# A two-layer encoder trunk on one core: attention values with v stationary, a router that works block by block, a longer warm-up and a split tail

## The chip, the cores and the metric

The kernel runs on one core of one Trainium2 chip, in one launch. The metric is the device time in microseconds of that core, the median over several executions. Lower is better.

## What is computed

The input x is 256 tokens of 1024 float32 channels. Two residual layers, each with a token mixer and a channel mixer, and a last RMSNorm:

```python
for i in range(2):
    hn = rms_norm(h, norm_mix[i])
    h = h + (fourier_mixer(hn, w_in, w_out) if i == 0 else neighbourhood_attention(hn, w_qkv, rpb, w_o))
    hn = rms_norm(h, norm_ffn[i])
    h = h + (swiglu(hn, ffn_gate, ffn_up, ffn_down) if i == 0 else moe_swiglu(hn, router_w, router_b, ...))
return rms_norm(h, final_norm)
```

Layer 0 mixes tokens and channels by a 2-D Fourier transform between two 1024x1024 projections, and then has a dense SwiGLU with 2816 hidden channels. Layer 1 has attention with 16 heads of 64 channels and a biased window, and then a mixture of 8 experts (3584 hidden channels each) of which every token takes its top 2. All of it is in float32.

## The kernel before

The program is written engine by engine (one block for each of SyncE, GpSimd, ScalarE, VectorE and TensorE), so the order on every engine is the order of the code, and semaphores join the engines. No scheduler moves anything.

**Weights.** All weights come in pieces of 128x2048 floats (1 MB, `raw`, a ring of 7, loaded by SyncE). For float32 accuracy each piece is split in two: ScalarE writes its rounded part (`w_hi`, L458), VectorE the remainder (`w_lo`, L753), both in rings of three (`SPLIT`). `split_past(n)` in the code of either engine makes all pieces up to n + 2 that aren't made yet. TensorE multiplies each tile in three products (`three`, L1250 to L1252: high by high, high by low, low by high). A piece is 12 products of 512 columns for one block of 128 tokens. Loading piece j waits until piece j - 7 is split.

**Stages.** `still` runs products of zeros (L1321) until the first data is there. Then `first_projection` and w_in, the Fourier transform (`token_dft` into bank T, `channel_dft` into bank Y, each alternating between two of the eight PSUM banks), w_out, the dense feed-forward part, qkv. The left operands `act_hi` and `act_lo` come from transposes of h, a quarter (two of the eight channel tiles) at a time; `stream_second` has TensorE wait for two quarters before it starts on them.

**Attention.** In a loop over 8 pairs of heads TensorE does the scores of pair p (L1512, 64 channels each, so the two heads sit in the upper and lower half of the array), the four transposes per head of the previous pair's probabilities (L1525), and the values of the pair before that (`head_values`, L1537: the transposed probabilities are the stationary operand, 64 columns of v the moving one). VectorE adds the bias (L951) and takes the maximum (L955), ScalarE copies transposed probabilities (`probT`, L625) and takes the exponentials (L630, four for a pair). VectorE divides eight heads at once by their sums (`output`, L933 and L936), and `outputs_transposed` (L1488) turns them by TensorE before the projection w_o (`wo_product`, pieces W0 to W0+3).

**Router.** After the last w_o product the second half of h is transposed for both token blocks, split into act_hi and act_lo, multiplied by the router's weights (L1578, L1585, 8 to 16 columns), and a chain of small VectorE instructions finds the two experts of each token and its slot. `keep_warm` (L1592) is filler: products of the identity with itself. Then the tokens of expert 0 are gathered by products with a 0/1 matrix (L1619), transposed, split, and the first gate product starts.

**Experts and end.** 8 experts of 42 pieces each. The last expert's result is scattered back (L1766, L1767), added to h (L1118), and the last norm and the four stores follow.

Of the kernel before, what the change touches and what calls it, by code (L numbers as in the profile page):

```python
# [26 lines left out]
P = 128  # L27
D = 1024
S = 256
# [96 lines left out]
def trunk(nc, x, norm_mix, norm_ffn, w_in, w_out, w_qkv, w_o, ffg, ffu, ffd, router_w, router_b,  # L126
# [47 lines left out]
    def layout(entries, off):  # L174

        made = {}
        for name, shape, dt in entries:
# [11 lines left out]
                       ("p_sum", [P, NB, HEADS], f32), ("p_inv", [P, NB, HEADS], f32)]  # L189
# [44 lines left out]
    def sem(name):  # L234
# [5 lines left out]
    lo_part, still_made = sem("lo_part"), sem("still_made")  # L240

# [19 lines left out]
    bias_done, a_score, a_biased, a_max, a_exp, a_inv, a_pT, a_pTcopy, a_pv, a_out, a_oT, a_ohi, a_olo, ao_psum = (sem(n) for n in (  # L261
        "bias_done", "a_score", "a_biased", "a_max", "a_exp", "a_inv", "a_pT", "a_pTcopy", "a_pv", "a_out", "a_oT", "a_ohi", "a_olo", "ao_psum"))

    sq_half, before_done, hnr_hi, hnr_lo, rw_hi_done, rw_lo_done, ones_done, logit_psum, low_added, gap_done, ratio_done, used_done, rank_psum, flag_done, dve_chain = (sem(n) for n in (
        "sq_half", "before_done", "hnr_hi", "hnr_lo", "rw_hi_done", "rw_lo_done", "ones_done", "logit_psum", "low_added", "gap_done", "ratio_done", "used_done", "rank_psum", "flag_done", "dve_chain"))
# [4 lines left out]
    e_y, fin_rstd, fin_done = (sem(n) for n in ("e_y", "fin_rstd", "fin_done"))  # L270
# [31 lines left out]

    def has_before(j, E, back):

        return E is not None or j >= back
# [3 lines left out]
    STREAM = [TY, TY, TY, [G[0], G[1], U[0], Y[0]]]  # L309
# [6 lines left out]
    OT = [U[0], Y[0], G[0], G[1]]  # L316
    WO = [[U[0], Y[0]], T]

    def HT(c):

        return G if c == DC - 1 else T

# [11 lines left out]
    def _(sp):  # L334
# [53 lines left out]
        for b in range(NB):  # L388
            for q in range(2):
                sp.wait_ge(fin_done, 2 * b + q + 1)  # L390
                cs = slice(BANK * q, BANK * (q + 1))
                sp.dma_start(out[0, P * b:P * (b + 1), cs], hn[:, b, cs]).then_inc(s_out, 16)
# [3 lines left out]
    def _(pool):  # L396
# [11 lines left out]

        pool.wait_ge(a_pv, HEADS)
# [8 lines left out]
        rstds(3)  # L418
# [22 lines left out]

        for b in range(NB):
            pool.wait_ge(sq_done, NB * 4 + b + 1)
            nc.gpsimd.tensor_scalar(rstd[:, 4, b:b + 1], sumsq[:, 4, b:b + 1], 1.0 / D, EPS, ALU.mult, ALU.add).then_inc(rstd_chain, 1)
            pool.wait_ge(rstd_chain, 4 + 1 + b + 1)
# [3 lines left out]
    def _(act):  # L449
        made = [0]  # L450

        def split_hi(j, E):
# [5 lines left out]
            nc.scalar.activation(w_hi[w][:], raw[s][:], ACT.Copy).then_inc(hi_made, 1)  # L458

# [25 lines left out]
        def squares(i):  # L485
# [3 lines left out]
            for b in range(NB):  # L489
                if i == 4:  # L490
                    act.wait_ge(e_added, b + 1)
                terms = mo["hn_hi"] if i == 4 else hn
# [40 lines left out]
        for g in range(GROUPS + 2):  # L533
            for m in (2 * g, 2 * g + 1) if g < GROUPS else ():
# [3 lines left out]
                nc.scalar.activation(fo["pt_hi"][:, m % PT], T[m % 2][:], ACT.Copy).then_inc(pt_hi_done, 1)  # L538
# [4 lines left out]
            if 1 <= g < GROUPS + 1:  # L543
# [3 lines left out]
                nc.scalar.activation(fo["odd"][:, (g - 1) % 2], Y[(g - 1) % 2][:, S:], ACT.Copy).then_inc(ft_odd, 1)  # L547
# [50 lines left out]
        def output_hi(q):  # L598
            act.wait_ge(a_oT, q + 1)
            nc.scalar.activation(act_hi[:, 2 * q:2 * q + 2], two(OT[q]), ACT.Copy).then_inc(a_ohi, 1)  # L600
# [14 lines left out]
        split_past(W0 - 2)  # L615
        for p in range(PAIRS + 1):
# [3 lines left out]
            if p:  # L620
                for g in (2 * p - 2, 2 * p - 1):
# [4 lines left out]
            if p < PAIRS:  # L626
                for i in (2 * p, 2 * p + 1):
# [9 lines left out]
            if 0 <= p - FIRST_PART < PARTS:  # L637
                split_part(W0 + 1, p - FIRST_PART)
        split_past(W0)
        output_hi(2)  # L640
        output_hi(3)
        split_past(W0 + 1)
        act.wait_ge(s_rout, 64)
        nc.scalar.activation(mo["rw_parts"][:, :, :NE], mo["rw"][:], ACT.Copy).then_inc(rw_hi_done, 1)
        split_past(W0 + 3)
        stream_hi(3, 0)

        def token_hi(c):

            cs = slice(BANK * c, BANK * (c + 1))  # L650
            for b in range(NB):
# [1184 lines left out]
```

## Time and profile before

| | |
|---|---|
| median of 3 executions | 1366.86 us (1364.64 to 1367.56) |
| the profiled execution's own time | 1367.15 us |
| its span in the trace | 1365.3 us |
| TensorE busy | 1344.7 us, 98% |
| VectorE busy | 1111.9 us, 81% |
| ScalarE busy | 923.2 us, 68% |
| GpSimd busy | 34.5 us, 3% |
| data moved | 432.32 MB, 317 GB/s on average |

A busy time is the union of an engine's instructions, with the ends of TensorE's pipelined instructions modelled; so the distance between starts tells more of TensorE than its busy share. Times in the rows below are from the start of the span.

### The profile page before, as it was taken

The numbers are of one execution on the slowest core, as the hardware profiler recorded it, in microseconds if no ns is written. First come the engines' busy times: TensorE is split into PE (matmuls) and PEld (weight loads), VectorE is DVE, ScalarE is ACT, GpSimd is POOL, SyncE is SP. The second block draws the span as 40 slices with busy tenths as digits, with TensorE's granted clock in tenths as the row PEclk, the third lists the DMA queues.
The fourth block names the chain that finished last, engine by engine and source line by source line (L and its number), as shares of the span: only waits on it lengthen the run. The fifth ranks groups of instructions, "written<-read, shape, count | busy, mean of one in ns | idle before, by whom it ended". The sixth has DMA issues, their size and how long they took to land.

```text
span 1365.3 us, 17406 instructions
## 1 busy us (share of the span) xinstructions
PE 1344.7 (98%) x6341; PEld 1117.9 (82%) x6341; DVE 1111.9 (81%) x815; ACT 923.2 (68%) x755; POOL 34.5 (3%) x48
## 2 busy tenths in 40 slices
PE   8999999999999999999999999999999999999997
PEld 7888888787878888888888888888888888888885
DVE  5756666655678889888988988898898889889997
ACT  6554444545647778777777877877787787777774
POOL 0000000000101000000000000000000000002000
PEclk8999999999989999999999999999999999999999
DMA  9666775563339999999999999999999999999992
GB/s 354 246 207 179 210 211 190 175 204 104 101 109 378 383 378 365 395 382 357 398 388 372 373 394 377 358 398 388 368 376 394 367 370 397 381 374 385 396 394 90
DMA packets 194971, 432.32 MB, mean 317 GB/s; under 512 B 19632, under 2 KB 22064, under 8 KB 194800
## 3 DMA queue, kind: packets, MB, share of 16 engines
q1 hardware_dynamic: 178784, 416.28, 83.4%
q0 software_dynamic: 3360, 11.78, 2.2%
q10 hardware_dynamic: 12784, 3.69, 1.8%
q8 instruction: 27, 0.44, 0.1%
q14 instruction: 16, 0.13, 0.0%
HBM read 425.94 MB, written 5.78 MB: 316 GB/s over the span
## 4 chain that ended last, share of the span: by engine, by line
PE 95%; DVE 3%; ACT 1%; issue 1%; DMA 0%; POOL 0%; DVEq 0%; ACTq 0%
PE bank_G L1250 10%; PE bank_G L1252 10%; PE bank_G L1251 10%; PE bank_U L1250 10%; PE bank_U L1252 10%; PE bank_U L1251 10%; PE bank_Y L1250 8%; PE bank_Y L1252 8%; PE bank_Y L1251 8%; PE bank_T L1696 2%; PE bank_T L1250 1%; PE bank_T L1252 1%; PE bank_T L1251 1%; DVE w_lo L753 1%; PE bank_G L1512 0%
## 5 line engine op out<-in xcount | busy, mean ns | idle before, releaser
L753 DVE TENSOR_TENSOR w_lo<-raw,w_hi 128x2048 fp32r<-128x2048 f32 x390 | 885.9, 2289 | 184.6 <-ACT w_hi L458 183.8
L458 ACT ACTIVATE w_hi<-raw 128x2048 fp32r<-128x2048 f32 x390 | 748.6, 1920 | 276.6 <-PE bank_U L1252 98.2
L1250 PE MATMUL bank_Y<-w_hi,hidT_hi 128*128 128x512 f32 x492 | 192.2, 391 | 0.0
L1252 PE MATMUL bank_Y<-w_hi,hidT_lo 128*128 128x512 f32 x492 | 191.6, 389 | 0.0
L1251 PE MATMUL bank_Y<-w_lo,hidT_hi 128*128 128x512 f32 x492 | 191.5, 389 | 0.0
L1250 PE MATMUL bank_U<-w_hi,xg_hi 128*128 128x512 f32 x448 | 179.1, 400 | 0.0
L1250 PE MATMUL bank_G<-w_hi,xg_hi 128*128 128x512 f32 x448 | 175.2, 391 | 1.3 <-DVE xg_lo L774 0.9
L1252 PE MATMUL bank_U<-w_hi,xg_lo 128*128 128x512 f32 x448 | 175.0, 391 | 0.0
L1251 PE MATMUL bank_U<-w_lo,xg_hi 128*128 128x512 f32 x448 | 174.5, 390 | 0.0
L1252 PE MATMUL bank_G<-w_hi,xg_lo 128*128 128x512 f32 x448 | 174.5, 390 | 0.0
L1251 PE MATMUL bank_G<-w_lo,xg_hi 128*128 128x512 f32 x448 | 174.4, 389 | 0.0
L1252 PEld LDWEIGHTS bank_Y<-w_hi,hidT_lo 128*128 128x128 f32 x492 | 92.4, 188 | 19.4
L1250 PEld LDWEIGHTS bank_Y<-w_hi,hidT_hi 128*128 128x128 f32 x492 | 92.3, 188 | 19.3
L1251 PEld LDWEIGHTS bank_Y<-w_lo,hidT_hi 128*128 128x128 f32 x492 | 92.4, 188 | 18.7
L1250 PEld LDWEIGHTS bank_G<-w_hi,xg_hi 128*128 128x128 f32 x448 | 84.1, 188 | 21.0 <-issue 2.9
L1252 PEld LDWEIGHTS bank_U<-w_hi,xg_lo 128*128 128x128 f32 x448 | 84.1, 188 | 18.3
L1252 PEld LDWEIGHTS bank_G<-w_hi,xg_lo 128*128 128x128 f32 x448 | 84.1, 188 | 17.7
L1251 PEld LDWEIGHTS bank_G<-w_lo,xg_hi 128*128 128x128 f32 x448 | 84.1, 188 | 17.1
L1251 PEld LDWEIGHTS bank_U<-w_lo,xg_hi 128*128 128x128 f32 x448 | 84.3, 188 | 16.3
L1250 PEld LDWEIGHTS bank_U<-w_hi,xg_hi 128*128 128x128 f32 x448 | 84.2, 188 | 15.9
L1250 PE MATMUL bank_G<-w_hi,act_hi 128*128 128x512 f32 (+1 forms) x176 | 68.6, 390 | 4.4 <-DVE w_lo L761 3.1
L1250 PE MATMUL bank_U<-w_hi,act_hi 128*128 128x512 f32 (+1 forms) x176 | 67.7, 384 | 0.3 <-DVE act_lo L774 0.3
(301 smaller groups left out, 1363.5 us busy)
## 6 DMA issues: line engine op xcount, KB each, us to landing
raw<-in_expert_w_gate SPq DMA_DIRECT2D x112, 1024.0 KB, 7.7
raw<-in_expert_w_up SPq DMA_DIRECT2D x112, 1024.0 KB, 7.8
raw<-in_expert_w_down SPq DMA_DIRECT2D x112, 1024.0 KB, 7.7
raw<-in_nat_w_qkv SPq DMA_DIRECT2D x12, 1024.0 KB, 5.1
raw<-in_ffn_w_gate SPq DMA_DIRECT2D x11, 1024.0 KB, 8.9
raw<-in_ffn_w_up SPq DMA_DIRECT2D x11, 1024.0 KB, 5.7
raw<-in_ffn_w_down SPq DMA_DIRECT2D x11, 1024.0 KB, 5.2
raw<-in_fourier_w_out SPq DMA_DIRECT2D x4, 1024.0 KB, 15.6
```

The costliest lines, as they stand in the source:

```text
L458: nc.scalar.activation(w_hi[w][:], raw[s][:], ACT.Copy).then_inc(hi_made, 1)
L753: nc.vector.tensor_tensor(w_lo[w][:], raw[s][:], w_hi[w][:].bitcast(f32), ALU.subtract).then_inc(lo_made, 1)
L1250: nc.tensor.matmul(out_, xh, wh, start=start, stop=False)
L1251: nc.tensor.matmul(out_, xh, wl, start=False, stop=False)
L1252: return nc.tensor.matmul(out_, xl, wh, start=False, stop=stop)
L1696: last = nc.tensor.transpose(T[c % 2][:, P * k:P * (k + 1)], hid[c % 2][:, P * k:P * (k + 1)], ident[:])
```

## The change

- `still(12)` becomes `still(23)`.
- The Fourier transform uses four banks for `token_dft` (BY_TOKEN) and four for `channel_dft` (BY_CHANNEL), and drops the waits that two banks needed.
- For gate column 0 and qkv column 0, TensorE waits for one quarter of `act_lo` at a time.
- Attention values: v (64 columns) is stationary and the transposed probabilities (256 columns) move, so the result of a pair comes out with channels on partitions, the two heads in the two halves of the partitions. The reciprocals of the sums (VectorE) are spread over 64 columns by GpSimd (`p_wide`), transposed by TensorE (two per pair), copied by ScalarE (`scale_copy`), and multiplied by VectorE (`scaled_values`). `outputs_transposed` is gone. ScalarE now alternates one probT copy and one head's two exponentials.
- Router: h is added, transposed, squared, split and multiplied for one block of tokens after the other; w_o products change their order. The gains are multiplied into the router's weights. Two weight pieces less are split ahead of the router. `keep_warm(6)` becomes 24, `keep_warm(2)` becomes 8.
- End: the last piece of the last expert is split in halves by columns; the first half of the result is scattered and added while the second is computed. The squares are taken by halves, and the last scaling is shared by VectorE and ScalarE.

```diff
-        still(12)
+        still(23)
...
-            if m >= 2:
-                pe.wait_ge(pt_lo_done, m - 1)
+            if m >= 4:
+                pe.wait_ge(pt_lo_done, m - 3)
...
+                        if stream is not None and b == 0 and kk % 2 == 0:
+                            pe.wait_ge(act_lo_done, 4 * stream + kk // 2 + 1)
...
+        for p in range(PAIRS):
+            pool.wait_ge(a_inv, p + 1)
+            if p >= 2:
+                pool.wait_ge(a_rT, p - 1)
+            nc.gpsimd.tensor_copy(att["p_wide"][:, p % 2].rearrange("p b (h d) -> p b h d", h=2),
+                                  att["p_inv"][:, p % 2].unsqueeze(3).to_broadcast([P, NB, 2, HD])).then_inc(a_wide, 1)
...
+        def pair_values(p):
+
+            pe.wait_ge(a_pTcopy, 2 * p + 2)
...
+            if p >= 2:
+                pe.wait_ge(a_out, p - 1)
+            for k in range(NB):
+                for half in range(2):
+                    g = 2 * p + half
+                    last = nc.tensor.matmul(values_of(p)[HD * half:HD * (half + 1)], att["v"][:, k, HD * g:HD * (g + 1)],
+                                            att["probT"][:, g % PROBS, S * k:S * (k + 1)], start=(k == 0), stop=(k == NB - 1))
+            last.then_inc(a_pv, 2)
+            pe.wait_ge(a_wide, p + 1)
...
+                last = nc.tensor.transpose(scales_of(p)[:, P * b:P * (b + 1)], att["p_wide"][:, p % 2, b], ident[:])
+            last.then_inc(a_rT, 1)
...
-        keep_warm(6)
+        keep_warm(24)
...
-        keep_warm(2)
+        keep_warm(8)
...
+                last_columns(0, 4)
+                last_columns(1, 2)
+                scatter(0)
+                last_columns(1, 2, 2)
```

On ScalarE, two passes through the attention loop, before: `hid` is the exponentials' output, `probT` the copies, `w_hi` a part of a weight piece.

```order
L625 ACTIVATE probT<-bank_T 128x512 x2
L630 ACTIVATE hid,p_sum<-silu_g,neg_max 128x256 x4
L470 ACTIVATE w_hi<-raw 128x512
L625 ACTIVATE probT<-bank_T 128x512 x2
L630 ACTIVATE hid,p_sum<-silu_g,neg_max 128x256 x4
L470 ACTIVATE w_hi<-raw 128x512
```

And the same place after the change:

```order
L661 ACTIVATE scale<-bank_U 128x256
L675 ACTIVATE probT<-bank_T 128x512
L680 ACTIVATE hid,p_sum<-silu_g,neg_max 128x256 x2
L675 ACTIVATE probT<-bank_T 128x512
L680 ACTIVATE hid,p_sum<-silu_g,neg_max 128x256 x2
L512 ACTIVATE w_hi<-raw 128x512
```

The second copy of a pass now stands between the exponentials of the two heads, and a copy of 256 columns is added.

On TensorE, from the last router product to the first gather product, before and after (`ident` alone is the filler, `used` the ranking of the tokens):

```order
L1585 MATMUL bank_G<-rw_parts,act_lo 128x8 x8
L1592 MATMUL bank_T<-ident 128x128 x6
L1610 MATMUL bank_T<-used,before_h 128x8
...
L1614 MATMUL bank_T<-used,ones 128x8
L1592 MATMUL bank_T<-ident 128x128 x2
L1619 MATMUL bank_G<-hn_hi,sel 128x512 x2
```

```order
L1677 MATMUL bank_G<-rw_parts,act_lo 128x8 x4
L1685 MATMUL bank_T<-ident 128x128 x24
L1717 MATMUL bank_T<-used,before_h 128x8
...
L1721 MATMUL bank_T<-used,ones 128x8
L1685 MATMUL bank_T<-ident 128x128 x8
L1726 MATMUL bank_G<-hn_hi,sel 128x512 x2
```

The filler ahead of the ranking grows from 6 products to 24, that behind it from 2 to 8.

On VectorE, behind the router, where the first gate's left operand (`xg_lo`) is made, before and after:

```order
L774 TENSOR_TENSOR xg_lo<-bank_U,xg_hi 128x512
L1201 TENSOR_REDUCE most<-bank_T 128x1
L753 TENSOR_TENSOR w_lo<-raw,w_hi 128x2048
L1205 SCALAR_TENSOR_TENSOR hn<-h,rstd,gain 128x1024 x2
L753 TENSOR_TENSOR w_lo<-raw,w_hi 128x2048
```

```order
L853 TENSOR_TENSOR xg_lo<-bank_U,xg_hi 128x512
L1301 TENSOR_REDUCE most<-bank_T 128x1
L825 TENSOR_TENSOR w_lo<-raw,w_hi 128x2048 x2
L1305 SCALAR_TENSOR_TENSOR hn<-h,rstd,gain 128x1024 x2
L825 TENSOR_TENSOR w_lo<-raw,w_hi 128x2048
```

One more weight piece (W0+5, the second of expert 0) is split here than before; it stood ahead of the router.

## Rows read from the trace of the kernel before

**Rows 1.** The page: shares of the chain that ended last.
```profile
PE 95%; DVE 3%; ACT 1%; issue 1%; DMA 0%; POOL 0%; DVEq 0%; ACTq 0%
```

**Rows 2.** Stretches: us, busy time of each engine, granted clock, DMA share, GB/s.
```profile
385.00:390.00 5.00, 3.56 (x29) 3.15 (x28) 4.49 (x13) 3.41 (x11) 0.54 (x2) 1.00 0.50 197
390.00:404.00 14.00, 12.28 (x59) 10.69 (x59) 9.02 (x33) 4.32 (x7) 1.26 (x2) 0.63 0.01 2
404.00:1354.00 950.00, 949.58 (x4328) 785.49 (x4326) 849.96 (x524) 719.92 (x482) 23.25 (x21) 1.00 1.00 372
```

**Rows 3.** Stretches at the start: L1321 alone (PE, PEld), then all PE.
```profile
1.00:4.33 3.33, 3.23 (x15) 3.23 (x16) 1.00 0.71 218
4.33:5.60 1.27, 1.24 (x11) 1.05 (x10) 1.00 0.72 187
...
7.75:14.57 6.82, 5.92 (x14) 0.50 1.06 405
14.57:22.30 7.73, 7.73 (x35) 1.00 1.03 388
```

**Rows 4.** Timeline around the Fourier transform, VectorE and PE.
```profile
27.67 4.68 DVE L753 TENSOR_TENSOR w_lo<-raw,w_hi 128x2048 fp32r<-128x2048 f32 x2
34.88 1.36 DVE L774 TENSOR_TENSOR pt_lo<-bank_T,pt_hi 128x512 fp32r<-128x512 f32 x2
37.15 0.28 PE L1250 MATMUL bank_Y<-pt_hi,dft_hi 128*128 128x256 f32 x1
```

**Rows 5.** PE's waits of 250 to 265 us: total, times, longest.
```profile
PE bank_G L1250 <- DVE act_lo L778: 1.4, 1, 1.4
```

**Rows 6.** Four attention pairs as one stretch; then timeline rows of one pair.
```profile
337.00:352.18 15.18, 15.18 (x129) 13.41 (x129) 11.87 (x20) 14.12 (x44) 0.00 (x0) 1.00 0.01 2
...
338.06 1.29 DVE L951 SCALAR_TENSOR_TENSOR silu_g<-bank_G,bias 128x512 f32<-128x512 f32 x2 [1.56 <-PE bank_G L1512]
338.65 1.09 ACT L625 ACTIVATE probT<-bank_T 128x512 f32<-128x512 f32 x2
339.27 1.27 DVE L955 TENSOR_REDUCE neg_max<-silu_g 128x2 f32<-128x512 f32 x2
339.98 0.51 ACT L630 ACTIVATE hid<-silu_g,neg_max 128x256 f32<-128x256 f32 x1 [0.24 <-DVE neg_max L955]
```

**Rows 7.** Timeline of PE: scores, transposes, one block's values, first w_o product.
```profile
348.36 1.13 PE L1512 MATMUL bank_G<-kT,qT 64*128 64x256 f32 x8
...
356.78 0.56 PE L1537 MATMUL bank_U<-v,probT 128*128 128x64 f32 x4
358.52 1.04 PE L1525 MATMUL bank_T<-ident,hid 128*128 128x128 f32 x8
359.84 0.50 PE L1250 MATMUL bank_U<-w_hi,act_hi 128*128 128x512 f32 x1 [0.28 <-DVE act_lo L774]
```

**Rows 8.** GpSimd's first instruction of 256 columns in the timeline.
```profile
0.74 0.31 POOL L404 MEMSET hid<- 128x256 f32 x1 [0.29 <-POOLq L1817]
```

**Rows 9.** Timeline of the router, PE and the last VectorE step of the choice.
```profile
385.40 0.51 PE L1578 MATMUL bank_G<-rw_parts,act_hi 128*128 128x16 f32 x4
393.09 2.91 PE L1592 MATMUL bank_T<-ident 128*128 128x128 f32 x12
396.39 0.17 DVE L1029 TENSOR_TENSOR used<-first,second 128x16 bf16<-128x16 f32 x1
398.17 1.22 PE L1619 MATMUL bank_G<-hn_hi,sel 128*128 128x512 f32 x2 [0.19 <-DVE sel L1074]
403.58 0.47 PE L1250 MATMUL bank_G<-w_hi,xg_hi 128*128 128x512 f32 x1 [0.90 <-DVE xg_lo L774]
```

**Rows 10.** VectorE's timeline behind the router.
```profile
404.14 2.29 DVE L753 TENSOR_TENSOR w_lo<-raw,w_hi 128x2048 fp32r<-128x2048 f32 x1
406.35 2.47 DVE L1205 SCALAR_TENSOR_TENSOR hn<-h,rstd,gain 128x1024 f32<-128x1024 f32 x2
```

**Rows 11.** VectorE's timeline at the end.
```profile
1359.98 2.74 DVE L1236 SCALAR_TENSOR_TENSOR hn<-h,rstd,gain 128x512 f32<-128x512 f32 x4 [1.42 <-POOL rstd L446]
```

More of the change, by code:

```diff
@@ L619, in _ @@
                 output_hi(1)
-            if p:
-                for g in (2 * p - 2, 2 * p - 1):
+            if p >= 3:
+                scale_copy(p - 3)
+            for half in range(2):
+                if p:
+                    g = 2 * p - 2 + half
                     act.wait_ge(a_pT, g + 1)
@@ L625, in _ @@
                     nc.scalar.activation(att["probT"][:, g % PROBS], T[g % 2][:], ACT.Copy).then_inc(a_pTcopy, 1)
-            if p < PAIRS:
-                for i in (2 * p, 2 * p + 1):
+                if p < PAIRS:
+                    i = 2 * p + half
                     act.wait_ge(a_max, i + 1)
@@ L967, in _ @@
         split_past(W0)
-        for b in range(NB):
-            output(1, b)
+        scaled_values(PAIRS - 2)
+        scaled_values(PAIRS - 1)
         output_lo(2)
@@ L1177, in expert @@
                         gather_copy(E + 2)
+                if (kind, c, half) == ("up", STEPS - 1, 0) and kept and not sweep:
+                    gate_weights()
                 if (kind, half) == ("down", 0) and kept and not sweep and 1 <= c < 5:
@@ L1252, in three, with project @@
             return nc.tensor.matmul(out_, xl, wh, start=False, stop=stop)
-        def project(pieces, banks, width, done, before=lambda n, b: None):
+        def project(pieces, banks, width, done, before=lambda n, b: None, stream=None):
             for n, j in enumerate(pieces):
@@ L1340, in token_dft @@
             for b in range(NB):
-                last = three(T[m % 2][:, S * b:S * (b + 1)], fo["u_hi"][:, b, o:o + P], fo["u_lo"][:, b, o:o + P],
+                last = three(BY_TOKEN[m % 4][:, S * b:S * (b + 1)], fo["u_hi"][:, b, o:o + P], fo["u_lo"][:, b, o:o + P],
                              fo["dft_hi"][:, b, 0:S], fo["dft_lo"][:, b, 0:S], True, True)
@@ L1480, in v_product @@
                 last.then_inc(qkv_psum, 1)
[L1482 to L1489 removed]
         def wo_product(c, half, b):
             pe.wait_ge(a_olo, 2 * half + 2)
+            if (c, half) == (0, 0):
+                pe.wait_ge(a_out, PAIRS - 3 + b)
             last = quarter(at["wo"][c][half], half, b, WO[c][b])
@@ L1592, in keep_warm, with last_wo_product @@
                 nc.tensor.matmul(T[0][:, :P], ident[:], ident[:], start=True, stop=True)
-        pe.wait_ge(rw_lo_done, 1)
-        pe.wait_ge(act_lo_done, 4 * 3 + 2)
-        for q in range(2):
-            logits_hi(q)
-            logits_lo(q)
-        transpose_stream(3, 1)
-        logits_hi(2)
-        logits_hi(3)
-        logits_lo(2)
-        logits_lo(3).then_inc(logit_psum, 1)
-        keep_warm(6)
+        def last_wo_product():
+            j = at["wo"][1][1]
+            ready(j, None)
+            wh, wl = parts(j, None, KH)
+            for k in range(KH):
+                if k == KH // 2:
+                    transpose_tokens_of(1, 0)
+                kk = KH + k
+                last = three(WO[1][1][:], act_hi[:, kk, P:], act_lo[:, kk, P:], wh[:, k], wl[:, k], False, kk == KD - 1)
+            last.then_inc(piece_used, 1)
+        wo_product(0, 1, 0)
+        wo_product(1, 1, 0)
+        transpose_tokens_of(0, 0)
+        wo_product(0, 1, 1)
+        transpose_tokens_of(0, 1)
+        last_wo_product()
+        pe.wait_ge(rw_lo_done, 1)
+        logits(0, 0)
+        logits(0, 1)
+        transpose_tokens_of(1, 1)
+        logits(1, 0)
+        logits(1, 1)
+        keep_warm(24)
         pe.wait_ge(used_done, 1)
```

392 lines of the change are left out of this document (230 added, 162 removed).

## The prediction

> **What bounds the kernel now.** I read the chain that ended last first: TensorE holds 95% of it [rows 1]. Then the stretches: from 404 to 1354 us, 70% of the span, TensorE is busy 949.58 of 950 us at full clock [rows 2]; and the change touches nothing in it. There a piece is 12 products of 512 columns, at about 0.225 us each (35 records begin in 7.73 us in [rows 3], and a few records can be missing), 2.7 us. So only TensorE's gaps and its half-clock stretches elsewhere can be won or lost. They are five: the start, the Fourier transform, one wait at 256 us, the attention stage with the router behind it, and the end. In each I ask which engine's result TensorE waits for, and what is late next when that wait is taken away. The sum below is made against the profiled execution's own 1367.15 us, which is 0.3 above the median.
>
> **Start and Fourier transform: −2.2.** Before, 24 filler instructions (two for each product) run from 1.1 us on, up to 4.33 at half clock (15 in 3.23 us, 0.213 each), then at full (11 in 1.24 us, 0.11 each; a stretch counts what crosses its border); then TensorE idles from 5.6 to 8.65 us, where the first weight piece is ready. The 14 products from 7.75 to 14.57 run at 0.50 of the clock, those behind at full clock [rows 3]; so 14 cost 14 × 0.21 = 2.9 us more. `still(23)` issues 46 instructions: 15 × 0.213, and 31 × 0.11 = 3.4, so it ends near 7.8 and leaves 0.9 us idle. Before, the clock was still full 2.2 us after the filler ended, so I take it as full from the first product on. That moves TensorE about 3 us ahead, but the next consumer is limited by VectorE: it makes two pieces of `w_lo` from 27.67 on, 4.68 us, and only later the first `pt_lo`, 34.88 to 36.24, without which the channel transform can't begin (37.15) [rows 4]. That VectorE work waits for TensorE only through `u_lo`, so it moves by about 1.3 us at the first `pt_lo` (ready 34.9 instead of 36.2); the four banks then take away a further 0.9 us of bank waits. I book 2.2 of at most 3.2. The bounds: 0 if the clock falls in the 0.9 us and VectorE stays where it is, −3.2 if nothing behind TensorE is late.
>
> **Quarter waits: −0.8.** TensorE waits 1.4 us for `act_lo` at 256.6 [rows 5]. The four instructions that make it (0.41 us each) are waited for as four; waiting for the first two saves two of them, 0.8. The bounds are 0 and −1.4. At qkv the same wait has slack already, so nothing.
>
> **Attention, steady pairs: 0.** Four pairs take 15.18 us, all TensorE; ScalarE has 14.12 of it busy [rows 6]. So a pair takes 3.8: scores 1.06, eight transposes 0.95 to 1.04, values 358.52 − 356.78 = 1.74 for four groups [rows 7]. After the change the values are eight instructions of 256 columns. In the trace 128 columns of such a product take 0.11 [rows 3], so one after another they would take 8 × 0.22 = 1.8, as before. But the scores are eight instructions of 256 columns too, and take 1.13 [rows 7], because the upper and the lower half of the array work at once. If the left and the right half do the same, the values take about 1.0, and with the two transposes of `p_wide` (0.28) TensorE's pair falls to 3.3. The Trainium skill's page "TensorEngine Tiling (Array Packing)", section Performance Considerations, names this very exchange, a small moving side made stationary together with column tiling, with up to 2× to be had. The same page, Key Properties, speaks against it: a change of tiling mode drains TensorE, and there would be one more change in each pair. By the first rule the values would take about 0.9, by the second some of it comes back; this case has a row for row halves only, and no run here shows column halves yet.
>
> What a pair can give is not TensorE's, though. Bias (0.65 a head), maximum (0.64), exponential (0.51 twice) and copy (0.55) hang in a ring [rows 6]: the bias of pair p + 1 writes `silu_g`, which the exponentials read. Before, the order is bias, maximum, two copies in the maximum's shadow, four exponentials. After, a copy stands between the two heads' exponentials: 0.6 + 0.65 + 1.0 + 0.5 + 1.0 and handovers of 0.24 or less are 3.95, above the 3.8 of before. Five pairs lose 0.13 each, the first pair wins 0.6 (no values in it, no pair of copies): 0.
>
> GpSimd's spreading of the reciprocals is hidden. It has no row; the nearest is its write of 256 columns, 0.31 us [rows 8], and its slack is a whole pair less two handovers, about 1.6 us. Above 1.6 each microsecond would delay a pair.
>
> **From scores(7) to the logits: +0.6.** Before, the first product with w_o starts 7.66 us after scores(7) (352.18 to 359.84) [rows 7]. After, bias of the last head starts 2.2 us after the scores do, and then stand in line 0.6 (bias), 0.7 (maximum), 1.0, 0.5, 1.0 (exponentials, copy, exponentials), 1.0 (`act_hi` twice, each as a copy of 512 columns), 0.4 (`scale_copy`), 0.4 (product with v's result), 0.1 (reciprocal) and 1.3 (`act_lo` twice, as `pt_lo`): 9.2 us, +1.5. The 0.4's are guesses between 0.31 and 0.55, as no row has 256 columns of these forms. Then it gives back: the values of heads 14 and 15 −0.55, no `outputs_transposed` in the second half −1.0; and three groups of four transposes now stand between w_o products where one of eight stood behind them, +0.65. The sum is +0.6. If the column halves do not overlap, 1.9 must be added.
>
> **Router: +0.2.** With t0 the end of the last w_o product (385.40), before has the logits at t0 + 7.9, `used` at 396.56, the ranking at t0 + 11.2, the gather at t0 + 12.8, the first gate product at t0 + 18.2 [rows 9]. At 390.04 the clock fell, and stayed at half to 400.28 (0.63 as a mean of the stretch to 404, 1.00 ahead of it [rows 2]). After, the logits are there at t0 + 4.8, since the transposes, splits and squares of block 0 lie behind w_o's own products, and the chain of small VectorE instructions (2.9 us) has `used` at t0 + 7.8. But TensorE first runs 48 filler instructions: 5.3 us at 0.11, 10.2 at 0.213 (12 took 2.91, which has two handovers in it [rows 9]). If the clock falls in the middle of them they take 7.75, the ranking starts at t0 + 12.5, the second filler (16) takes 1.8 and the gather starts at t0 + 14.4. From gather to gate were 5.4 us; 1.4 of them is the half clock up to 400.28, so 4.0 remain: t0 + 18.4. So the gain of the logits (3.1 us) goes into filler that is longer than the work it covers.
>
> **Expert 0: +1.5.** VectorE after the router has one `w_lo` of 2.29 us, then `hn` twice, 2.47 us, then the next `w_lo` [rows 10]. After the change two pieces are split ahead of `hn`, W0+5 and W0+6, so W0+7, the fourth of the expert, is ready at 0.56 + 2 × 2.21 + 2.47 + 2.29 = 9.7 behind the gate's start (VectorE begins 0.56 behind it, and the pieces' starts are 2.21 apart), and TensorE wants it three pieces behind it, at 8.2. Before the slack was 0.7. Wait 1.5. If VectorE starts it while TensorE still gathers, 0.7; bound 2.3.
>
> **End: −0.8.** The adds end 0.5 later by halves, but the squares behind them are taken half by half, and the last scaling (four in 2.74 us on VectorE [rows 11]) is shared with ScalarE: −1.3.
>
> **Sum:** 1367.15 − 2.2 − 0.8 + 0.6 + 0.2 + 1.5 − 0.8 = 1365.65 for the profiled execution, and 0.3 less against the median: 1365.4.
>
> **The rivals.**
> A. As above: 1365.4, with 1363.6 to 1366.8 by half the terms' bounds. For it speaks that the clock fell at t0 + 4.6 before, with TensorE idle in pieces ahead of it (3.56 busy of 5 us [rows 2]), which the new order leaves in part. Chance 0.40.
> B. The clock holds all through the router, because the w_o products, transposes and filler follow each other without idle time: filler 5.3, ranking at t0 + 10, gate at t0 + 15.8, −2.6 on A: 1362.8. Against it: the products of 8 and 16 columns keep TensorE's clock no longer than 4.6 us in the trace of before. Chance 0.25.
> C. The column halves do not overlap, or each change of shape costs what the overlap gives: +1.9, 1367.3. For it: no row shows them overlapping. Against it: row halves do. Chance 0.20.
> D. Slower than before: the clock is half through the whole filler and the gather. Then ranking at t0 + 15, gather at t0 + 18.4, gate at t0 + 23.8: +5.4 on A, 1370.8. Each filler instruction at half clock costs 0.1 more: from 15 more than in A the kernel is no longer faster, and only with all of both fillers and part of the gather at half (+4.3) is it slower by over 0.2%. Chance 0.15.
> GpSimd as the bound of the pairs (over 2 us a spreading) is in D's chance, too, at +1 to +2 in eight pairs.
>
> **Numbers.** A measurement of this kernel tells from no change about 0.2%, 2.7 us. Faster by that (under 1364.1): most of B and a third of A, 0.36. Slower by that (over 1369.6): most of D, 0.14. The rest, 0.50. The range leaves out 1 in 10 on either side: from B's lower part, 1360.8, to between C and D, 1368.8.
>
> **What would show it.** At the start: clock 1.00 from 7.75 to 14.57, and the first channel product near 35. At 256: a wait of 0.6. In attention: pairs 3.95 apart, value instructions 0.11 to 0.14 apart if halves overlap and 0.22 if not, and the w_o gap at scores(7) + 9.2. In the router: `used` long done when the ranking starts, the filler its releaser, and the place of the clock's fall. In expert 0: a wait of about 1.5 on `w_lo` before the fourth piece. At the end: last `hn` 0.8 closer to the last product. Most likely to make me wrong is the clock in the router, 5 us from best to worst; next the overlap of the halves, 1.9.

## The result and the profile after

| | before | changed kernel |
|---|---|---|
| median | 1366.82 us (20 executions) | 1369.22 us (20 executions) |
| lowest and highest | 1364.64, 1368.03 | 1367.35, 1370.16 |
| profiled execution, its span | 1367.15, 1365.3 | 1367.38, 1365.6 |

The ratio is 1.0019 with a 95% interval of 1.0012 to 1.0025: 1.6 to 3.4 us slower, where a gain of 1.4 was forecast. The changed kernel's executions fall into two groups, five from 1367.35 to 1367.80 and fifteen from 1368.75 to 1370.16. The mean granted clock is on record for each: 0.996 or 0.997 in the five, 0.995 in eleven of the fifteen and 0.996 in four. The profiled one is of the lower group, so its trace doesn't show what the median has; the profiles of the variants do (below). One of the eleven executions of e8 (below) took 1687.20 us at a mean granted clock of 0.75, and its ratio leaves it out.

The table follows TensorE through three traces: before, the changed kernel (lower group), and e7 (below), the same kernel but for who issues two stores, profiled in the upper group. Times are starts in the timeline.

| start of | before | changed | e7 |
|---|---|---|---|
| first channel product | 37.15 | 34.42 | 34.95 |
| first qkv product | 258.36 | 254.93 | 255.46 |
| scores(0) | 320.20 | 316.77 | 317.29 |
| scores(7) | 352.18 | 349.01 | 349.54 |
| first w_o product | 359.84 | 358.22 | 358.75 |
| last w_o product | 385.17 | 382.76 | 384.85 |
| ranking | 396.62 | 394.75 | 396.83 |
| first gate product | 403.58 | 401.09 | 403.18 |
| 37th product with xg_hi (fifth piece) | 415.93 | 415.05 | 417.11 |
| end of the span | 1365.26 | 1365.57 | 1367.92 |

The changed kernel is 3.4 us ahead at the scores, 2.5 at the first gate product, 0.9 in the fifth piece of expert 0, and 0.3 behind at the end. The start: the stretches that answer to [rows 3], TensorE alone.

```profile
7.75:14.57 6.82, 6.82 (x38) 1.00 1.06 405
14.57:22.30 7.73, 7.73 (x36) 1.00 1.03 388
```

The products there run at full clock now. The attention's last passes, in the timeline (start, duration, engine, line, operation, count, and in brackets the idle time before and who ended it); [rows 6, 7] show the same of before.

```profile
347.63 1.08 PE L1633 MATMUL bank_U<-probT,v 128*64 128x256 f32 x8
348.64 0.44 PE L1640 MATMUL bank_U<-ident,p_wide 128*128 128x128 f32 x2
349.01 1.14 PE L1606 MATMUL bank_G<-kT,qT 64*128 64x256 f32 x8
350.05 0.40 POOL L434 COPY p_wide<-p_inv 128x256 f32<-128x256 f32 x1 [3.57 <-DVE p_inv L1012]
...
354.01 1.08 PE L1633 MATMUL bank_U<-probT,v 128*64 128x256 f32 x8 [0.95 <-ACT probT L675]
354.85 1.14 ACT L640 ACTIVATE act_hi<-hn 128x512 fp32r<-128x512 f32 x2
355.30 1.04 PE L1619 MATMUL bank_T<-ident,hid 128*128 128x128 f32 x8
356.28 0.42 DVE L1017 TENSOR_TENSOR hn<-bank_Y,scale 128x256 f32<-128x256 f32 x1 [2.92 <-ACT scale L661]
356.70 1.46 DVE L853 TENSOR_TENSOR act_lo<-hn,act_hi 128x512 fp32r<-128x512 f32 x2
358.22 0.50 PE L1352 MATMUL bank_U<-w_hi,act_hi 128*128 128x512 f32 x1 [1.89 <-DVE act_lo L853]
```

Eight value products of 256 columns take 1.08 us. In the trace they start in pairs, 0.01 us apart, and a pair follows the other after 0.21 to 0.26: the left and the right half of the array do work at once. Still, scores(6) and (7) start 3.97 us apart where it was 3.82, and TensorE waits twice before the w_o product. The stretches that answer to [rows 2], all engines (PE, PEld, DVE, ACT, POOL, granted clock, DMA, GB/s):

```profile
350.00:358.22 8.22, 5.10 (x38) 3.08 (x36) 4.87 (x10) 7.55 (x22) 1.58 (x3) 1.00 0.41 131
358.22:366.00 7.78, 7.78 (x38) 5.81 (x39) 4.34 (x5) 3.06 (x5) 3.38 (x6) 1.00 0.39 120
382.99:388.62 5.63, 5.01 (x45) 4.91 (x44) 3.23 (x10) 3.23 (x4) 1.64 (x3) 1.00 0.00 0
388.62:392.04 3.42, 3.42 (x18) 3.42 (x18) 2.00 (x13) 1.69 (x2) 0.00 (x0) 0.50 0.01 2
392.04:401.09 9.05, 8.15 (x68) 7.41 (x66) 4.32 (x11) 1.44 (x3) 0.00 (x0) 1.00 0.01 2
```

TensorE is busy 5.10 of the 8.22 us ahead of the w_o product. The router's rows, which answer to [rows 9]:

```profile
387.68 7.23 PE L1685 MATMUL bank_T<-ident 128*128 128x128 f32 x48
390.75 0.17 DVE L1127 TENSOR_TENSOR used<-first,second 128x16 bf16<-128x16 f32 x1
394.75 0.17 PE L1717 MATMUL bank_T<-used,before_h 128*128 128x8 bf16 x1
396.66 0.71 PE L1726 MATMUL bank_G<-hn_hi,sel 128*128 128x512 f32 x2
401.09 0.47 PE L1352 MATMUL bank_G<-w_hi,xg_hi 128*128 128x512 f32 x1 [0.90 <-DVE xg_lo L853]
```

`used` is there at 390.92, and the ranking starts 3.8 us later, with no wait shown: TensorE is still in its own filler. TensorE's waits from 350 to 420 us (in all, times, longest) add the one in expert 0, to set beside [rows 10]:

```profile
PE bank_U L1352 <- DVE act_lo L853: 1.9, 1, 1.9
PE bank_U L1352 <- DVE w_lo L825: 1.0, 1, 1.0
```

And the end, where [rows 11] stood; L1335 multiplies by the gain, L1338 and L809 scale by `rstd`:

```profile
1356.76 0.75 DVE L1216 SCALAR_TENSOR_TENSOR h<-bank_T,weight,h 128x512 f32<-128x512 f32 x1 [0.88 <-PE bank_T L1859]
1358.20 1.29 DVE L1335 TENSOR_TENSOR hn<-h,gain 128x512 f32<-128x512 f32 x2
1358.44 1.10 POOL L478 TENSOR_SCALAR rstd<-sumsq,sumsq_half 128x1 f32<-128x1 f32 x1 [1.71 <-ACT hn_hi L805]
1360.23 0.77 DVE L1338 SCALAR_TENSOR_TENSOR hn<-h,rstd,gain 128x512 f32<-128x512 f32 x1 [0.74 <-POOL rstd L480]
1360.55 0.86 POOL L480 TENSOR_TENSOR rstd<-rstd,half_power 128x1 f32<-128x1 f32 x1
1361.03 2.03 SPq L413 DMA_DIRECT2D out<-hn  x4
1361.45 0.75 DVE L1338 SCALAR_TENSOR_TENSOR hn<-h,rstd,gain 128x512 f32<-128x512 f32 x1 [0.45 <-POOL rstd L480]
1361.51 0.72 ACT L809 ACTIVATE hn<-hn,rstd 128x512 f32<-128x512 f32 x1 [0.49 <-POOL rstd L480]
```

The last hn is ready at 1362.23, 0.5 earlier than before, and yet the span ends 0.3 later. But the kernel came to its end 0.9 ahead: counted from the 37th product with xg_hi, the last hn is 0.4 later than before. The first store is issued at 1361.03, before at 1360.77; counted the same way, it is 1.1 later.

### The profile page after: what moved, and what is told of

Read it like the earlier page. It is cut to its first block, busy times and chain, and to the rows that moved or that the text cites. A ratio compares the mean times of both kernels' runs of the same rounds, so it can differ in the third digit from the quotient of the medians.

```text
span 1365.6 us, 17478 instructions
## 1 busy us (share of the span) xinstructions
PE 1344.4 (98%) x6347; PEld 1111.2 (81%) x6347; DVE 1113.0 (82%) x823; ACT 926.3 (68%) x766; POOL 37.6 (3%) x59
## 4 chain that ended last, share of the span: by engine, by line
PE 92%; DVE 3%; ACT 2%; DMA 1%; issue 1%; SPq 0%; POOL 0%; POOLq 0%; DVEq 0%; ACTq 0%
PE bank_U L1352 10%; PE bank_G L1352 10%; PE bank_U L1354 10%; PE bank_U L1353 10%; PE bank_G L1354 10%; PE bank_G L1353 10%; PE bank_Y L1352 8%; PE bank_Y L1354 8%; PE bank_Y L1353 8%; PE bank_T L1803 2%; DVE w_lo L825 1%; DMA raw<-in_fourier_w_in 1%; PE bank_T L1354 1%; PE bank_T L1352 1%; PE bank_T L1353 1%
## 5 line engine op out<-in xcount | busy, mean ns | idle before, releaser
L1354 PEld LDWEIGHTS bank_U<-w_hi,xg_lo 128*128 128x128 f32 x448 | 84.1, 188 | 18.3
```

The source lines that it names most:

```text
L1354: return nc.tensor.matmul(out_, xl, wh, start=False, stop=stop)
```

## The experiments

Each kernel is the changed one with one edit, timed in several rounds beside the kernel before. Ratios are to the kernel before; the changed kernel's is 1.0019.

**e1: the end of before.** Pieces, adds, squares and scaling as in the kernel before; the core of it:

```diff
-                last_columns(0, 4)
-                last_columns(1, 2)
-                scatter(0)
-                last_columns(1, 2, 2)
+            down(STEPS - 1, 0)
+            down(STEPS - 1, 1)
```

> The changed kernel with the end of the kernel before (last piece whole, adds, squares and last scaling as before). The prediction's theory: the new end saves 0.8 us, so undoing it gives 1369.2 + 0.8 = 1370.0. Theory read from the two traces: from the fourth gate piece of expert 0 on, the changed kernel is 0.88 us ahead and at the end of the span 0.31 behind, so the new end costs 1.2 us, because the last two halves of hn are ready within 0.03 us of each other and their stores are issued one behind the other on SyncE; undoing it gives 1368.0, and the span ends about 2.5 us behind the last hn, not 3.3.

Median 1368.27, ratio 1.0013 (1.0004 to 1.0022), so the interval overlaps the changed kernel's. The trace tells more: from the 37th product with xg_hi to the end of the span are 949.18 us, 949.33 in the kernel before, and 950.52 in the changed one (950.46 to 950.80 in the six variants that keep its end unchanged). The new end costs 1.1 to 1.6 us, against a forecast gain of 0.8.

**e2: `still(12)` again.**

```diff
-        still(23)
+        still(12)
```

> The changed kernel with still(12) again. Theory: the longer filler gives 2.7 us at the first channel product, of which 0.9 belongs to the four banks; undoing the filler costs 1.8 to 2.7, so 1371.0 to 1371.9. The executions of the changed kernel fall into two groups, 1367.4 to 1367.8 and 1368.8 to 1370.2. If the groups come from the clock in the router, both stay, 1.7 us apart. Rival: they come from whether the clock survives the start's filler; then one group is left.

1369.69, ratio 1.0022 (1.0013 to 1.0031). The first channel product starts at 34.94 with the short filler, and in the other variants with the long one and four banks at 34.79 to 35.36. So the filler moves the w_in products (the Fourier transform begins at 31.86, in the others by 31.4) and nothing behind them, within what is measured. Two groups of executions remain, two of eleven in the lower. I expected 1.8 to 2.7 us and that was wrong.

The profile is of the upper group. The w_o products take 24.50 us at full clock; the clock is half in the router, for 6.83 us instead of the changed kernel's 3.41. From the last w_o product to the first gate product are 19.94 us instead of 18.33:

```profile
387.84:394.67 6.83, 6.83 (x34) 6.83 (x34) 2.61 (x15) 2.97 (x3) 0.00 (x0) 0.50 0.00 1
```

**e3: a shorter filler ahead of the ranking.**

```diff
-        keep_warm(24)
+        keep_warm(10)
```

> The changed kernel with 10 filler products ahead of the ranking instead of 24. Theory: the filler is what the ranking waits for (used is done at 390.92, the ranking starts at 394.75), so it starts 3.5 us earlier and the time is 1369.2 - 3.5 = 1365.7. Rival: the clock stays at half through the gather, which takes back 1.5 to 2: 1367.4. Rival 2: with 28 instructions less the clock falls in all executions for two stretches, and nothing is gained in the upper group: 1369.

1366.41, ratio 0.9997 (0.9988 to 1.0006), clear of the changed kernel's interval: 0.22% or 3.0 us by the ratios. The ranking starts at 393.38, right behind `used` (393.06). Its profile also shows what the changed kernel's own didn't. Stretches of e3 around the first w_o products, then the middle one of them in the changed kernel:

```profile
359.00:360.00 1.00, 1.00 (x5) 0.82 (x6) 0.07 (x1) 0.90 (x1) 0.00 (x0) 1.00 0.00 0
360.00:363.41 3.41, 3.41 (x11) 2.20 (x11) 2.56 (x2) 0.00 (x0) 0.00 (x0) 0.50 0.00 0
363.41:366.00 2.59, 2.59 (x16) 1.81 (x17) 0.66 (x2) 1.18 (x3) 1.25 (x2) 1.00 0.84 279
```

```profile
360.00:363.41 3.41, 3.41 (x20) 2.23 (x19) 2.24 (x3) 0.71 (x2) 0.79 (x1) 1.00 0.15 14
```

TensorE is busy all through, but in e3 at the lower of its two clocks (0.50, 1.2 GHz) for 3.4 us, behind the stretch in which it waited twice: 11 products begin there, 20 in the changed kernel. From the first to the last w_o product are 24.54 us in the changed kernel and 26.05 in e3: 1.5 us. The medians of the two groups are 1.7 apart (1367.63 and 1369.36).

**e4: W0+5 split while VectorE waits for the ranking.**

```diff
         nc.vector.tensor_tensor(mo["gap"][:], ...)
+        split_past(W0 + 3)
```

> The changed kernel with piece W0+5 split on VectorE right behind used and gap, where VectorE is idle until the ranking at 394.75. Theory: the wait of 1.2 us on w_lo before the fourth piece of expert 0 and the 0.2 before the second go away and nothing else moves: 1369.2 - 1.4 = 1367.8. Rival: the split's 2.3 us make hn_lo or the slots late: 1369.2 or more. Rival 2: the wait only moves to a later piece of expert 0 and nothing is gained: 1369.2.

1367.78, ratio 1.0012 (1.0003 to 1.0021). The wait on `w_lo` is gone from the trace, and from the first gate product to the 37th with xg_hi pass 12.37 us instead of 13.96, as before the change (12.35). The 1.4 expected is what the medians give; the ratios' intervals overlap.

**e5: filler in the gap ahead of w_o.**

```diff
         head_transposes(HEADS - 1)
+        for _ in range(8):
+            nc.tensor.matmul(G[1][:, 3 * P:4 * P], ident[:], ident[:], ...)
         wo_product(0, 0, 0)
```

> The changed kernel with 8 filler products (identity by identity) behind the last transposes of the attention, where TensorE waits 2.1 us for act_lo before the first product with w_o. Nothing waits less. Theory: in most executions of the changed kernel the clock falls to half for 3.4 us around 359 to 363, just behind that wait (seen in three of four profiles of its variants, not in its own), and costs 1.6 us; with the filler it doesn't fall, the upper group of executions is gone, and the median is 1369.2 - 1.6 = 1367.6. Rival: the clock falls because of the earlier wait too (1.2 us at 353); then the two groups stay and the median is 1369.2.

1369.17, ratio 1.0017 (1.0008 to 1.0026): no gain, and two groups as before. Its profile, of the upper group, shows the clock full behind the first w_o product and then half in the router for twice as long as in the changed kernel, as e2's does:

```profile
358.63:366.00 7.37, 7.37 (x36) 5.48 (x37) 4.35 (x5) 2.65 (x5) 2.97 (x5) 1.00 0.35 101
386.25:393.07 6.82, 6.36 (x30) 6.27 (x30) 3.65 (x18) 4.47 (x5) 0.66 (x1) 0.50 0.01 4
```

Whether the filler kept the clock up there can't be told from one profile, as the changed kernel and e2 had it full there without. The theory (a gain of 1.6) fell: the second half-clock stretch is in this execution all the same, in the router. The rival's number is right, but its reason, that the clock falls in the tail, isn't what the profile shows.

**e6: the left operand of w_o earlier.**

```diff
-        scaled_values(PAIRS - 3)
-        pair_scales(PAIRS - 1)
         output_lo(0)
         output_lo(1)
+        scaled_values(PAIRS - 3)
+        pair_scales(PAIRS - 1)
```

and on ScalarE `output_hi(0)` moves between the last pair's exponentials.

> The changed kernel with act_hi and act_lo of the first four channel tiles made earlier: ScalarE copies the first in the idle 0.67 us ahead of the last pair's exponentials, VectorE makes both act_lo ahead of the scaling of pair 5. Theory: the wait of 2.1 us before the first w_o product is an order on ScalarE and VectorE and not a need; the product starts right behind the transposes, about 1.9 us earlier, and the clock doesn't fall either: 1369.2 - 1.9 - 1.6 = 1365.7, if the w_o stage behind it has no wait of its own. Rival: the w_o stage waits for pieces of w_lo or for the second half of act_lo instead; then only the clock's 1.6 is won: 1367.6.

1367.36, ratio 1.0007 (0.9998 to 1.0016). The w_o product starts at 356.84, 7.2 us behind scores(7), not 9.2, and there is no wait on `act_lo` ahead of it. So that wait was an order on two engines and no need. By the ratios 1.6 us came of the 3.5 expected, with intervals that overlap: the executions still spread from 1365.73 to 1369.71. The profile, one of the three fastest (to 1365.99, the next is 1366.95), has 3.41 us of half clock, all in the router.

**e7: two of the stores issued by ScalarE.**

```diff
+            act.wait_ge(fin_scaled, b + 1)
+            nc.scalar.dma_start(out[0, P * b:P * (b + 1), BANK:], hn[:, b, BANK:]).then_inc(s_out, 16)
```

> The changed kernel with the two stores of the second column half issued by ScalarE behind its scaling instead of by SyncE. Theory: the new end is late because two halves are ready at once and SyncE needs about 0.7 us from one store to the next; with two queues the span ends 0.7 us earlier: 1368.5. Rival: the rest of the end's cost is in GpSimd's chain of three steps for the two rstd (1.1 us for the first), and the store's own time of 2.5 us behind the last hn is the same: 1369.2.

1370.05, ratio 1.0027 (1.0017 to 1.0038), and in the trace 3.33 us from the last hn to the end, as with one queue (3.34). My theory of e1, one store queued behind the other on SyncE, fell.

**e8: two banks each for the Fourier transform, and their waits.**

```diff
-            if m >= 4:
-                pe.wait_ge(pt_lo_done, m - 3)
+            if m >= 2:
+                pe.wait_ge(pt_lo_done, m - 1)
```

> The changed kernel with two banks each for token_dft and channel_dft again, and their waits. Theory: with still(12) the first channel product started at 34.94, within what still(23) gave (34.42 to 35.15), so the filler gives nothing and the banks about 0.9 of bank waits: 1370.1. Rival: the banks give the whole 2.1 us of the start: 1371.3. Rival 2: VectorE is the limit either way, and nothing is lost: 1369.2.

1370.13, ratio 1.0027 (1.0018 to 1.0036), 1.1 us above the changed kernel by the ratios, though the intervals overlap. The first channel product starts at 35.64.

**e9: the last half of hn 0.7 us later.** The added copy's result is not used.

```diff
             act.wait_ge(fin_rstd, b + 1)
+            if b:
+                nc.scalar.activation(mo["hn_hi"][:, b, BANK:], hn[:, b, BANK:], ACT.Copy, ...)
```

> The changed kernel with one more copy of 512 columns (0.7 us, its result unused) on ScalarE ahead of the last scaling, so the last half of hn is ready 0.7 us later and the first three are not. Theory from e7 and the traces: the four stores are 1.05 MB, and from the issue of the first to the end of the span 4.49, 4.54 and 4.55 us pass whatever the last hn does, so the end is set by the first half of hn and nothing changes: 1369.2, span minus first issue 4.55. Rival: the last half of hn sets the end: 1369.9 and 5.3.

Ratio 1.0019 (1.0010 to 1.0028), as the changed kernel. The last hn is ready 2.73 us ahead of the end instead of 3.34, and from the first issue to the end are 4.54 us:

```profile
1363.40 2.17 SPq L413 DMA_DIRECT2D out<-hn  x4
```

The stores' transfers show why. In both traces they begin 0.86 us behind the first issue and fill the DMA engines without a break until 0.8 us before the end. The changed kernel, then e9; the last two figures are the DMA share and GB/s:

```profile
1361.89:1364.78 2.89, 0.00 (x0) 0.00 (x0) 0.31 (x1) 0.34 (x1) 0.00 (x0) 0.50 0.94 363
```

```profile
1364.26:1367.15 2.89, 0.00 (x0) 0.00 (x0) 0.31 (x1) 0.95 (x2) 0.00 (x0) 0.50 0.94 363
```

So the last half of hn had 0.6 us to spare; the first store, with the transfers behind it, set the end.

**e10: four edits together.** e6, the end of before, `keep_warm(10)` and `keep_warm(4)`, and hn of block 0 made ahead of `tokens_lo(1, 1)`:

```diff
         squares_of_rest(1)
...
+        nc.vector.scalar_tensor_tensor(out=hn[:, 0], in0=h[:, 0], scalar=rstd[:, 3, 0:1], in1=mo["gain"][:, 0], ...)
         tokens_lo(1, 1)
```

> The changed kernel with four things undone or moved: act_hi and act_lo of the first channel tiles early (as e6), filler of 10 and 4 products instead of 24 and 8 (as e3), the end of the kernel before (as e1), and hn of the first token block made on VectorE ahead of the last router operand, where VectorE waits 1.3 us, instead of between two weight pieces of expert 0. Theory: the single results, each against its own runs of the kernel before, add up: the changed kernel is 2.4 above it, e6 takes 1.9, e3 2.5, e1 0.7, and hn 1.1 (the wait on w_lo shrinks from 1.2 to about 0.35): 3.8 us below the kernel before, 1363.0. Rival: the changes meet on the same waits, and half of it comes: 1365.

1360.78, ratio 0.9956 (0.9943 to 0.9970): 6.0 us faster than the kernel before, 2.2 more than expected. Of the expected sum only e6, e3 and e1 had been measured; the earlier hn was an estimate, and `keep_warm(4)` never ran alone. The router of e10:

```profile
387.26 4.49 PE L1679 MATMUL bank_T<-ident 128*128 128x128 f32 x20
391.58 0.17 PE L1711 MATMUL bank_T<-used,before_h 128*128 128x8 bf16 x1
...
392.91 0.73 PE L1720 MATMUL bank_G<-hn_hi,sel 128*128 128x512 f32 x2
397.34 0.47 PE L1346 MATMUL bank_G<-w_hi,xg_hi 128*128 128x512 f32 x1 [0.90 <-DVE xg_lo L844]
```

From ranking to gather pass 1.3 us, with 16 filler instructions it was 1.9 to 2.2; from the first gate product to the 37th with xg_hi 12.77. The ranking starts 1.1 us behind `used` (390.51), for the filler still outlasts it.

Beside e7's trace, which has the changed kernel's stages in the upper group, the 8.5 us come as follows: scores(7) to the first w_o product 2.0, the w_o products at full clock 1.6, from the last of them to the first gate product 2.5, from there to the 37th with xg_hi 1.2, the end 1.5, less 0.3 of a later start.

**e11: as e10 with 2 and 2 filler products.**

> As e10 with 2 and 2 filler products. Theory: the ranking can't start before used is made, 3.4 us behind the logits, so less filler only makes TensorE idle there, the clock stays at half longer, and the gather takes 1 to 1.5 us more: 1 to 1.5 above e10. Rival: the filler doesn't matter once it is shorter than the work on VectorE: as e10.

1360.74, ratio 0.9956 (0.9942 to 0.9969): the time of e10, as the rival said. The trace is another. From TensorE's last filler to the ranking are 2.9 us (starts at 386.89 and 389.78), and the ranking starts right behind `used` (389.72), 1.8 us earlier than in e10. But the clock is half until 394.35, through the gather (in e10 until 391.48), and from gather to gate product pass 5.92 us instead of 4.43. So the loss that the theory expected is there, 1.5 us, and the earlier ranking pays for it: that the times are equal is two amounts that cancel.

**e12: e10 with ScalarE's old order**, both copies and then four exponentials.

```diff
                     nc.scalar.activation(att["probT"][:, g % PROBS], T[g % 2][:], ACT.Copy).then_inc(a_pTcopy, 1)
...
+            for half in range(2):
                 if p < PAIRS:
```

> As e10, with ScalarE's old order in the attention loop: both copies of transposed probabilities, then the four exponentials. Theory of the prediction: the copy between the two heads' exponentials is what makes a pair 3.95 to 3.98 us long (bias, maximum, two exponentials, copy, two exponentials in a ring); without it a pair takes 3.8, bounded by ScalarE's own work, and five pairs and the way to the first w_o product give 0.8 to 1.5 us: 1359.3 to 1360.0. Rival: TensorE then waits for the copies, which come no earlier than before while its values start behind them, and a pair stays at 3.97: 1360.8.

1359.69, ratio 0.9946 (0.9933 to 0.9960), the lowest median here, 7.4 us below the kernel before; the interval overlaps e10's. Two passes of PE and ScalarE in its timeline:

```profile
344.99 1.13 PE L1601 MATMUL bank_G<-kT,qT 64*128 64x256 f32 x8
...
347.35 1.09 ACT L671 ACTIVATE probT<-bank_T 128x512 f32<-128x512 f32 x2
...
348.70 1.13 PE L1601 MATMUL bank_G<-kT,qT 64*128 64x256 f32 x8
```

A pair takes 3.71 us, 3.97 with the copy between the exponentials, and 3.82 in the kernel before. The w_o product starts 1.6 us earlier than in e10, but the w_o products then take 25.12 us instead of 24.50, and at the end of the span 0.7 us is left.

## Why the prediction was wrong

It forecast 1365.4 and faster; the kernel takes 1369.2. Two steps failed: the end, booked at −0.8, costs 1.2, and the sum has one stretch of half clock behind the attention where most executions have two, 1.5 us more. Step by step, in the trace of the profiled execution:

- **Start, −2.2:** −2.7 in this execution, −2.0 to −2.4 in most variants. The size held, the working didn't: with the short filler the same start came (e2), where VectorE goes from two weight pieces (27.50 to 32.37) through `u_lo` to `pt_lo` without a wait for TensorE; before, it waited 1.19 us for `u_hi`. Banks give about 1.1 of it by the ratios, whose intervals overlap (e8; its first channel product is 0.3 to 1.2 later than the others'). In e2 the clock was at half for 3.4 us at the start and in the profile of before for 6.8 with the same filler, so part of the 2.2 may be that one execution of before; that stays open. The kernel before isn't one time either: of its 33 executions beside e1, those with a mean clock of 0.994 took 1364.4 to 1366.3 us, those with 0.992 (as the profiled one) 1366.6 to 1367.7.
- **Quarter wait, −0.8:** from the first channel product to the first qkv product −0.7.
- **Steady pairs, 0:** scores(0) to scores(7) took 32.24 instead of 31.98, +0.3. The ring was the right bound (3.95 forecast, 3.97 measured), and e12 shows it by taking the copy out. The win of 0.6 booked against it was 0.3.
- **Scores(7) to the logits, +0.6:** first w_o product 9.2 behind scores(7), as forecast to 0.1; w_o gave 0.8 back. Together +0.8 at full clock.
- **Column halves:** they overlap (eight in 1.08 us): a pair of products every 0.21 to 0.26 us, about what the prediction reckoned for one (0.22). The Trainium skill's page "TensorEngine Tiling (Array Packing)", section Performance Considerations, lists this exchange with 2× column tiling, and the trace agrees. From the last value product to `p_wide` are 0.31 us, 0.1 more than from pair to pair; no experiment separates what that pays for. The Trainium skill says on the same page, section Key Properties, that a change of tiling mode drains TensorE, and this may be its price here. The new order has two more such changes in a pass (into the values and out of them), not the one that the prediction counts.
- **Router, +0.2:** last w_o product to the first gate product 18.33 instead of 18.41, with the filler as what the ranking waited for, and the clock down once in its middle: forecast right in its sum, with luck, as two parts cancel. The ranking came 0.7 earlier than forecast (11.8 behind the end of the last w_o product, not 12.5), and from gather to gate product were 4.4, not 4.0: the prediction took 1.4 off for the half clock from 398.17 to 400.28, and 2.1 us at half clock can cost 1.1 at most. The filler's price is now known: e3 makes it 3.0 us of needless filler.
- **Expert 0, +1.5:** +1.6 (13.96 instead of 12.35), undone by e4. The fourth piece starts 9.7 behind the gate's start, as forecast.
- **End, −0.8: the first step that failed.** It cost 1.2. The +0.5 for the adds held (0.48, counted from the 37th product with xg_hi). Of the −1.3 behind them the halved squares gave 0.4 and the shared scaling 0.8, as booked; but a path that the sum has at nothing took 1.1 back: GpSimd's roots, for which the scaling waits. From the last square to the last root are 2.48 us instead of 1.40, as GpSimd's chain began with a step of 1.10 us that took 0.19 before (read from the two traces; no run changed this chain alone). So the last hn comes 0.4 later behind the same work, not 0.8 earlier.

  The other 0.8 is the stores': from the last hn to the end 3.34 us instead of 2.53, since the prediction timed the last half of hn alone. The end has two limits: the last hn plus 2.5 us (2.53 in before, 2.50 and 2.51 in e1 and e10, whose first issue is 5.0 before the end), and the issue of the first store plus 4.5 (4.54 to 4.55 in the changed kernel, e7 and e9, whose last hn is 2.7 to 3.3 before it; 4.53 to 4.69 in the others with that end). The kernel before met both at once (2.53, 4.49); e12 meets neither closely (2.74, 5.24).

  In the new end the first store comes 1.1 later behind the same work and the last hn 0.4. Where the first store loses its 1.1 is at the scatter (y by selT) around the last product, first before, then changed:

```profile
1353.93 0.39 PE L1252 MATMUL bank_Y<-w_hi,hidT_lo 128*128 128x512 f32 x1
1354.46 0.47 PE L1766 MATMUL bank_T<-y_hi,selT 128*128 128x512 f32 x1
1355.73 0.50 PE L1766 MATMUL bank_T<-y_hi,selT 128*128 128x512 f32 x1
```

```profile
1351.96 0.47 PE L1858 MATMUL bank_T<-y_hi,selT 128*128 128x512 f32 x1
1354.12 0.40 PE L1354 MATMUL bank_Y<-w_hi,hidT_lo 128*128 128x512 f32 x1
1356.02 0.47 PE L1858 MATMUL bank_T<-y_hi,selT 128*128 128x512 f32 x1 [1.50 <-DVE y_lo L853]
```

  Before, the first half's four scatter products ran in the 1.80 us between the start of the last product and the second half's scatter, while `y_lo` was made; now they stand ahead of the last products, and of the same 1.90 us TensorE idles 1.50. So everything on block 0's path is 1.1 later, and from the end of its last add to the first store are 3.52 us in both traces: the halved squares and the shared scaling gave that path nothing.
- **The clock behind scores(7): the second, one half-clock stretch too few.** The sum has the clock fall once, in the router. It priced the new wait ahead of w_o at its 1.5 us and put a fall there at nothing. The profiles of the two lower groups (the changed kernel's and e6's) have one such stretch of 3.41 us from scores(7) to the first gate product. Those of e1 to e5, e8 and e9, all from the upper group of their executions, and that of e7, whose executions show no lower group, have two. In six (e1, e3, e4, e7 to e9) one of the two is in the w_o products, which take 26.0 to 26.1 us instead of 24.5; in e2 and e5 both are in the router, and from the last w_o product to the first gate product are 19.9 and 19.5 us instead of 18.3. The mean clocks of the executions agree: one stretch more lowers the mean by 0.5 × 3.41 / 1366 = 0.0012, and 0.9966 and 0.9953 are the averages of the two groups. Fifteen of twenty executions of the changed kernel are in the upper.

The two, +2.0 and +1.5 in most executions, are 3.5 of the 3.8 us that separate 1369.2 from 1365.4; the pairs' 0.3 is most of the rest. Shown are the 1.2 of the end (e1, and its parts in the two traces) and the price of the second stretch, 1.2 to 1.6, in the traces that have it. What brings it stays open. The wait ahead of w_o is the suspect for its place: of eight profiles that keep that wait without filler six have the fall behind it, of the five others none. But filler in the wait (e5) left the median where it was, without the wait (e6) only three of eleven executions are in the lower group (to 1365.99, the others from 1366.95), and e10 to e12 have two stretches in the router. That e10 gave more than was expected is, by the stretches, mostly the w_o products at full clock, 1.6 us; which of its edits did that wasn't taken apart.

## What to carry to other kernels

Where a stage has TensorE wait in short pieces, allow for one more stretch at half clock (1.2 to 1.6 us here), and look at more than one execution: a profile of the faster group doesn't show it. Filler that outlasts the work it covers becomes the bound; here 14 products less gave 3.0 us. When two engines share a last step, follow also the engine that feeds both: GpSimd's chain took back what halving and sharing had won. At this kernel's end two limits hold, the last result and the first store with all the bytes behind it: an edit that makes the first store later loses, whatever it does for the last, and work moved out of a wait to ahead of the last products is no longer free.

## What was not expected of the hardware

Where the half clock fell, and whether it lasted 3.4, 6.8 or 10.2 us, differed between executions of nearly the same program, and so did their times, by 1.5 us and more. GpSimd's spreading of the reciprocals took 0.39 or 0.40 us in seven pairs, near its row for a write of that size (0.31), and 0.78 in the last. A GpSimd operation on one column took 0.19 and 0.20 us with constants; with a second column as an operand it took 1.10 us the first time and 0.26 the second.
